# A hybrid decoder layer on one core: the pooling map inside the output weight, loads on other queues, and VectorE's attention step in another order

## The reference, cut to what matters

```python
z = rmsnorm(h, g_attn_norm) @ w_in            # columns: q 512, k 128, v 128, u 512
a = sliding_window_sink_attention(rms(q), rms(k), v, sinks, rel_bias)   # 8 heads, window 128
# four channel groups of 128, trailing means over 2/4/8/16 positions minus the token:
m = concat_g(pooled_g @ w_pool[g]) * pool_scale
h = h + concat(a, m) @ w_out                  # w_out: 1024 x 1024, rows 512.. belong to m
h = h + (silu(hn @ w_gate) * (hn @ w_up)) @ w_down          # hn = rmsnorm(h), d_ff 2816
h = h + sigmoid(rmsnorm(h) @ w_ple_gate) * (p @ w_ple_proj)
```

## Time and profile before

| | us |
|---|---|
| median of 3 runs | 2050.03 (2048.8 to 2052.91) |
| profiled execution, its own time | 2053.4 |
| its span, first to last instruction | 2051.5 |
| TensorE busy | 2011.2 (98%) |
| VectorE busy | 1372.9 (67%) |
| ScalarE busy | 899.7 (44%) |
| GpSimd busy | 406.5 (20%) |
| mean granted TensorE clock | 0.998 of full speed |

### The profile page before, as it was taken

How to read it: one execution, slowest core, us unless ns; L and a number is a source line. 1 busy time by engine, 2 the same in 40 slices (tenths; PEclk the granted TensorE clock), 3 DMA queues, 4 the chain that set the end, 5 groups by cost and what they waited for, 6 DMA issues and landing times.

```text
span 2051.5 us, 26122 instructions
## 1 busy us (share of the span) xinstructions
PE 2011.2 (98%) x9546; PEld 1663.4 (81%) x9546; DVE 1372.9 (67%) x1920; ACT 899.7 (44%) x1460; POOL 406.5 (20%) x508
## 2 busy tenths in 40 slices
PE   8999999999999999999999999999999999999998
PEld 6887878877788888888888878788888888888877
DVE  4696674767696665655888765966566566987663
ACT  4575754657433333333333543533333333334542
POOL 4454644645410000000000220000000000001310
PEclk9999999999999999999999999999999999999999
DMA  7757566364934223225825128432322328352143
GB/s 193 201 180 245 188 236 219 130 236 131 347 127 130 81 72 103 72 72 171 307 62 165 36 72 223 143 119 67 96 85 72 100 79 292 130 159 78 42 134 103
DMA packets 197387, 292.09 MB, mean 142 GB/s; under 512 B 16139, under 2 KB 118452, under 8 KB 195980
## 3 DMA queue, kind: packets, MB, share of 16 engines
q1 hardware_dynamic: 172672, 212.97, 34.1%
q0 software_dynamic: 22176, 76.96, 10.8%
q10 hardware_dynamic: 2412, 0.50, 0.1%
HBM read 223.25 MB, written 67.51 MB: 142 GB/s over the span
## 4 chain that ended last, share of the span: by engine, by line
PE 84%; DVE 6%; DMA 3%; issue 3%; ACT 2%; POOL 1%; SPq 0%; ACTq 0%; DVEq 0%; POOLq 0%
PE bank L2623 13%; PE bank L2627 13%; PE bank L2625 13%; PE bank L2660 7%; PE bank L2661 7%; PE bank L2662 7%; PE bank L2323 4%; PE bank L2325 4%; PE bank L2324 4%; PE bank L2299 2%; PE bank L2301 2%; PE bank L2300 2%; DMA w_parts<-w_split 1%; PE bank L2392 1%; DVE w_lo L1554 1%
## 5 line engine op out<-in xcount | busy, mean ns | idle before, releaser
L2623 PE MATMUL bank<-a_hi,ring_hi 128*128 128x512 f32 x1232 | 479.7, 389 | 1.0 <-DVE ring_lo L1917 0.7
L2627 PE MATMUL bank<-a_hi,ring_lo 128*128 128x512 f32 x1232 | 479.3, 389 | 0.0
L2625 PE MATMUL bank<-a_lo,ring_hi 128*128 128x512 f32 x1232 | 479.3, 389 | 0.0
L2623 PEld LDWEIGHTS bank<-a_hi,ring_hi 128*128 128x128 f32 x1232 | 231.3, 188 | 49.9 <-DVE ring_lo L1917 1.4
L2625 PEld LDWEIGHTS bank<-a_lo,ring_hi 128*128 128x128 f32 x1232 | 231.3, 188 | 48.0
L2627 PEld LDWEIGHTS bank<-a_hi,ring_lo 128*128 128x128 f32 x1232 | 231.3, 188 | 47.8
L2660 PE MATMUL bank<-d_hi 128*128 128x512 f32 x616 | 239.8, 389 | 0.0
L2662 PE MATMUL bank<-d_hi,d_lo 128*128 128x512 f32 x616 | 239.7, 389 | 0.0
L2661 PE MATMUL bank<-d_lo,d_hi 128*128 128x512 f32 x616 | 239.6, 389 | 0.0
L1376 ACT ACTIVATE d_hi<-keep 128x1024 fp32r<-128x1024 f32 x132 | 139.8, 1061 | 201.9 <-PE bank L2662 184.9
L975 POOL DMA_DIRECT2D hidden_T<-hid x88 | 47.6, 541 | 770.4 <-DVE hid L1953 750.7
(11 more groups left out here) (258 smaller groups left out, 3879.9 us busy)
## 6 DMA issues: line engine op xcount, KB each, us to landing
w_parts<-w_split POOLq DMA_DIRECT2D x88, 512.0 KB, 4.8
hidden_T<-hid POOLq DMA_DIRECT2D x88, 256.0 KB, 2.3
raws<-in_w_gate SPq DMA_DIRECT2D x80, 256.0 KB, 4.7
raws<-in_w_up SPq DMA_DIRECT2D x80, 256.0 KB, 5.1
keep<-hidden_T SPq DMA_DIRECT2D x66, 256.0 KB, 3.8
raw<-in_w_ple_gate SPq DMA_DIRECT2D x64, 256.0 KB, 4.2
keep<-in_w_down SPq DMA_DIRECT2D x44, 256.0 KB, 4.4
other<-hidden_T SPq DMA_DIRECT2D x44, 256.0 KB, 6.8
```

The lines of the kernel that those rows point to most:

```text
L2623: mm(dst[:, :], wh[:, g, cols], a_hi[o][:, k, :], start=fresh and k == 0, stop=False, skip_group_check=True)
L2625: mm(dst[:, :], wh[:, g, cols], a_lo[o][:, k, :], start=False, stop=False, skip_group_check=True)
L2627: ins = mm(dst[:, :], wl[:, g, cols], a_hi[o][:, k, :], start=False, stop=k == 3, skip_group_check=True)
```

## The change

- Ahead of everything else in the output projection, z(0) makes W_g · diag(s_g) · Wout_g: POOL loads rows 512 and up of `w_out` (`load_pooled_rows`, 4 x 512 KB), ACT and DVE scale and split them, TensorE multiplies (`mix_rows`, 24 matmuls), ACT copies the banks, POOL stores 4 x 512 KB to `w_mixed`. The out panels with r >= 2 are read from there, and `pool_y` and its copies and waits are gone.
- The constants are issued by POOL, gains 1 and 2 among them; ACT waits for the first gain alone, and issues a small activation at the very start. TensorE runs 12 matmuls on zeroed tiles before its first panel (`WARM`).
- `load_parts` is on SP. Some loads of SP change places (x chunks and h of tile 1, the `load_a` group).
- DVE's attention step: q is staged before `softmax_in`, v at j = 3, the pooled means at steps 4, 7, 11, 15; u copies go behind the hosted step unless the step begins a new pair. ACT keeps a copy of transposed k (`k_raw`), so that TensorE's next transpose waits for ACT and not for DVE.
- In the gate of even tiles the turn of the squares, the sum and the normalisation move one panel later, and ACT splits the panel for r = 1 between the squares.

```diff
STEPS = 4 * NB + LAG_PV
-SUMS_AT = {3: ((0, 0),), 5: ((1, 0), (1, 1)), 7: ((2, 0),), 8: ((2, 1), (2, 2)), 10: ((3, 0), (3, 1)),
-   11: ((3, 2),), 12: ((3, 3),)}
-MEAN_AT = {4: 0, 6: 1, 9: 2, 13: 3}
-REST_AT = {5: 0, 7: 1, 10: 2, 14: 3}
...
+SUMS_AT = {3: ((0, 0),), 5: ((1, 0), (1, 1)), 8: ((2, 0),), 9: ((2, 1), (2, 2)), 12: ((3, 0), (3, 1)),
+   13: ((3, 2),), 14: ((3, 3),)}
+MEAN_AT = {4: 0, 7: 1, 11: 2, 15: 3}
+REST_AT = {5: 0, 8: 1, 12: 2, 16: 3}
+POOLED_HI_AT, POOLED_LO_AT = {10: 0, 11: 1, 12: 2, 13: 3}, {11: 0, 12: 1, 13: 2, 14: 3}
+POOLED_AT, POOLED_COPY_AT = {13: 0, 14: 1, 15: 2, 16: 3}, {14: 0, 15: 1, 16: 2, 17: 3}
+POOLED_STORE_AT = {16: (0, 1), 17: (2,), 18: (3,)}
...
+WARM = 12
...
 kT_hi = sb("kT_hi", [P, (NB + 1) * P], RING0, F32R)
+wo_raw = [sb(f"wo_raw{g}", [P, D], 22 + 4 * g) for g in range(NPOOL)]
+wo_lo = [sb(f"wo_lo{g}", [P, D], 22 + 4 * g, F32R) for g in range(NPOOL)]
...
     def load_out(t, c):
         if t == 0:
+            if c == 0:
+                sp.wait_ge(mixed_stored, 16 * NPOOL)
             load(OUT_AT[t] + c, out_panel(c))
...
             heads = w_out[0:QW, :].rearrange("(j c p) n -> j p c n", j=2, p=HEAD_DIM)
             return [heads[j, :, 2 * r:2 * r + 2, cols] for j in range(2)]
-        return rows(w_out, 2 * r, 2 * r + 2, cols)
+        return rows(w_mixed[:, :], 2 * r - 4, 2 * r - 2, cols)
...
+    def load_parts(i):
+        kept = (10 + i - OUT_AT[1] if OUT_AT[1] <= i < Z_AT[3] else i - Z_AT[2] if i < Z_AT[3] else
+                i - Z_AT[3] if i < OUT_AT[2] else 10 + (i - OUT_AT[2]) % 8)
+        if i == SPLIT_END:
+            sp.wait_ge(lo_done, SPLIT_END)
+        elif i < SPLIT_END + SLOTS_W:
+            sp.wait_ge(panel_used, SPLIT_END)
+            for parity in range(2):
+                sp.wait_ge(parts_stored[parity], 16 * (SPLIT_END - KEPT_FROM))
+        else:
+            sp.wait_ge(panel_used, i - SLOTS_W + 1)
+        sp.wait_ge(parts_stored[kept % 2], 32 * (kept // 2 + 1))
...
+        for part in range(2):
+            sp.dma_start(w_parts[parts_slot(i)][:, part, :].bitcast(F32), w_split[kept, part]
+                           ).then_inc(parts_landed[parts_slot(i)], 16)
...
             else:
-                sp.wait_ge(y_done, 16)
                 sp.wait_ge(attn_lo, 32)
...
     for t in range(NT - 1):
         for c in range(10):
             load_z(t + 1, c)
+            if t == 1 and c == 0:
+                load_parts(Z_AT[2] + 1)
+            if t:
+                load_parts(Z_AT[t + 1] + c + 2)
...
+            if t == 1 and c == 9:
+                for k in range(4):
+                    load_chunk(3, k)
+                for b in range(NB):
+                    load_h(1, b)
...
         for c in range(8):
...
+            if t == 0 and c == 7:
+                load_parts(Z_AT[2])
+            if t:
+                load_parts(OUT_AT[t] + c + 2)
             if t < 2:
                 for k in {3: (4,), 4: (5, 6), 5: (7,)}.get(c, ()):
                     load_chunk(t + 2, k)
...
+        if OUT_AT[3] + c + 2 < ROW_PANELS:
+            load_parts(OUT_AT[3] + c + 2)
...
         if c == 1:
             load_a(0, 0)
+            load_a(0, 2)
+        if c == 2:
             load_a(0, 1)
             load_a(0, 3)
-        if c == 2:
-            load_a(0, 2)
...
     def z_section(t):
...
-            if t == 2 and half == 0:
-                load_parts(Z_AT[2] + 1)
-            if t >= 2 and half % 2 == 0:
-                load_parts(Z_AT[t] + half // 2 + 2)
...
                 if half == 7:
                     store_band()
                     powers(NORM1[0])
+                    load_pooled_rows()
...
+            if t == 0:
+                for g in POOLED_STORE_AT.get(half, ()):
+                    store_mixed(g)
...
-            if t == 0 and half == 14:
-                load_parts(Z_AT[2])
-            if t and half % 2 == 0 and OUT_AT[t] + half // 2 + 2 < ROW_PANELS:
-                load_parts(OUT_AT[t] + half // 2 + 2)
...
+    def load_constants():
+        pool.dma_start(rel_sb[0:N_BUCKETS, :], rel_bias).then_inc(consts, 16)
...
+        pool.dma_start(gains[:, 1, :], g_ffn).then_inc(consts, 16)
+        pool.dma_start(gains[:, 2, :], g_ple).then_inc(consts, 16)
...
+    def load_pooled_rows():
+        pool.wait_ge(consts, CONSTS)
+        for g in range(NPOOL):
+            pool.dma_start(wo_raw[g][:, :], w_out[QW + g * P:QW + (g + 1) * P, :]).then_inc(consts, 16)
...
+    def store_mixed(g):
+        pool.wait_ge(mixed_copied, 2 * g + 2)
+        pool.dma_start(w_mixed[g * P:(g + 1) * P, :], mixed[g][:, :]).then_inc(mixed_stored, 16)
...
     nc.gpsimd.memset(u[:, :, 0:CARRY], 0.0).then_inc(constants_set, 1)
+    load_constants()
...
             act.wait_ge(kcarried, s)
+        if n:
+            act.wait_ge(kstaged, n)
+        nc.scalar.activation(k_raw[:, :], bank[5][:, 0:P], ACT.Copy)
         nc.scalar.activation(kT_hi[:, (b + 1) * P:(b + 2) * P], bank[5][:, 0:P],
...
-    def pool_y_hi(s, g):
-        act.wait_ge(y_done, 4 * s + g + 1)
-        nc.scalar.activation(mix_of(s)[0][:, 4 + g, :], pool_bank(s, g)[:, :], ACT.Copy,
-                             scale=scale_sb[:, g:g + 1]).then_inc(y_hi, 1)
+    def pooled_rows_hi(g):
+        if g == 0:
+            act.wait_ge(consts, CONSTS + 16 * NPOOL)
+        nc.scalar.activation(wo_hi[g][:, :], wo_raw[g][:, :], ACT.Copy,
+                             scale=scale_sb[:, g:g + 1]).then_inc(wp_hi_done, 1)
+    def copy_mixed(g):
+        for e in range(2):
+            act.wait_ge(mixed_bank, 2 * g + e + 1)
+            nc.scalar.activation(mixed[g][:, e * T:(e + 1) * T], mixed_bank_of(g, e)[:, :],
+                                 ACT.Copy).then_inc(mixed_copied, 1)
...
+            if t == 1 and half == 5:
+                act.wait_ge(mixed_stored, 16 * NPOOL)
             for b in COPY_Q_AT[t > 0].get(half, ()):
...
         else:
-            for j in range(4, KC):
-                square_late(g + 1, j)
+            square_late(g + 1, 4)
+            square_late(g + 1, 5)
+            split(ple + 3)
+            square_late(g + 1, 6)
+            square_late(g + 1, 7)
...
-                if split_behind(second, e, r):
+                if split_behind(second, e, r) and (second or e or r):
...
+                    if r == 3:
                         spread(NORM3[g + 1], bank[BS0[1]], spread3)
...
-    act.dma_start(gains[:, 2, :], g_ple).then_inc(gain_landed, 16)
-    act.wait_ge(gain_landed, 48)
+    act.wait_ge(constants_set, 1)
+    nc.scalar.activation(neg_max[:, 0, 0:1], minus_half[:, :], ACT.Copy)
+    act.wait_ge(gain_landed, 16)
...
     for k in range(2):
         square(NORM1[0], k, h[:, k, :], sq)
-    load_constants()
...
+        nc.vector.tensor_tensor(kT_lo[:, cols], k_raw[:, :], kT_hi[:, cols].bitcast(F32),
                                 ALU.subtract).then_inc(kstaged, 1)
...
             dve.wait_ge(bias_landed, 16 * BIAS_LOADS)
+        if j == 3 and b + 1 < NB:
+            stage_q(s, b + 1)
         if has_unit(k, 0):
             first = P if s == 0 and b == 0 else 0
             softmax_in(16 * s + k, j, first)
-        if j == 3 and b + 1 < NB:
-            stage_q(s, b + 1)
...
+        if j == 3 and b < NB:
             stage_v(s, b)
         if j == 1 and b + 1 < NB:
...
-    def pool_y_rest(s, g):
...
+    def pooled_rows_lo(g):
+        dve.wait_ge(wp_hi_done, g + 2)
...
-            for g in U_COPY_AT[t > 0].get(half, ()):
+            fresh = any(has_unit(k, 0) and k % 2 == 0 for _, k in hosted_steps("z", t, half))
+            u_first = fresh or half == 19 or not late
+            for g in U_COPY_AT[t > 0].get(half, ()) if u_first else ():
                 copy_u(t, g)
             if half in QK_MEAN_AT.get(t, {}):
                 qk_mean(t, QK_MEAN_AT[t][half])
             if half == {0: 19, 3: 17}.get(t):
                 qk_normalise(t, 0)
-            if t:
-                for g in POOL_Z_COPY.get(half, ()):
-                    pool_y_rest(t - 1, g)
+            if t == 0 and half in POOLED_LO_AT:
+                pooled_rows_lo(POOLED_LO_AT[half])
+            if t == 1 and half == 5:
+                dve.wait_ge(mixed_stored, 16 * NPOOL)
             hosted("z", t, half, Z_AT[t] + half // 2 + 1 if half % 2 == 0 and late else None)
+            for g in () if u_first else U_COPY_AT[t > 0].get(half, ()):
+                copy_u(t, g)
...
-                    if r == 1:
+                    if r == 2:
                         sum_squares(NORM3[g + 1], bank[BS0[0]])
-                    if r == 2:
+                    if r == 3:
                         normalise3(g + 1, 0)
                         normalise3(g + 1, 1)
                         norm3_lo(g + 1, 0)
-                    if r == 3:
                         norm3_lo(g + 1, 1)
                 if not second and e == 1 and r == 1:
...
-        pe.wait_ge(kstaged, 4 * s + min((k + 1) // PAIRS + 1, NB))
+        pe.wait_ge(k_hi_done, 4 * s + min((k + 1) // PAIRS + 1, NB))
...
```

(38 more changed lines are left out.)

119 lines of the change are left out of this document (39 added, 80 removed).

## The result

The changed kernel takes 2065.85 us (median of 4 runs, 2064.62 to 2070.63) beside 2051.47 for the kernel before (4 runs, 2048.8 to 2054.97): ratio 1.0069, 95% interval [1.0054, 1.0084], 14.2 us slower. 2025.0 was forecast, with a range of 2015 to 2040 and 0.05 for slower. The profiled execution has a span of 2064.4 us.

What follows compares the result with a forecast made beforehand. TensorE, busy 98% of the span, was taken as the bound, so only fewer products or less standing help. The terms -6.4 - 2.3 + 1.0 - 4.0 - 6.5 - 3.0 + 1.0 - 4.8 made -25.0 us: 2050.0 to 2025.0, range 2015 to 2040.

Steps and rivals of the forecast that it cites:

- Step 6: Split-weight loads moved from POOL to SP: -3.0 us of late-load waits, and +1.0 for SP's order, bounds 0 and +4.
- second rival: One queue is too little: split-weight loads behind SP's other transfers each take 11.89 us; 2070 us, chance 0.05.
- Step 1: Pooling maps removed from 16 groups, -12.3 us; 24 products come instead, 5.9 us; net -6.4 us of TensorE.
- Step 2: Kernel start: earlier first panel -1.3 us, zeroed-tile products -2.0, waiting for panel 2 +1.0; sum -2.3 us.
- Step 3: Making the pooled weights in z(0), with 2 MB more to load: +1.0 us, bounds 0 and +5.
- Steps 4 and 5: Step 4: waits on the pooling result go, -4.0 us; step 5: DVE's attention step regrouped, -6.5, bounds 0 and -8.7.
- first rival: Waits move instead of vanishing: the attention step gives -2.5 us, pooled rows cost +5; 2033, up to 2040; chance 0.22.
- Step 7: Gate of tiles 0 and 2: waits on squares and late panels go, -5.1 us, +0.3 for DVE's load; sum -4.8.

Runs made afterwards that it cites:

- order mended: Kernel before with split-weight loads on SP, chunks 4 to 7 ahead, tile 1's h behind the third out panel's load, tile 2's stores together: 2051.2 us, ratio 0.9992.
- rows early: Changed kernel with the pooled rows of the output weight issued by GpSimd at half 4 of z(0): 2062.2 us, ratio 1.0048; other kernels include this edit.
- chunks first: Changed kernel with x chunks 4 to 7 of tile 3 issued ahead of the split weights of out(1)'s panels 2 and 3: 2050.3 us, ratio 0.9991.
- chunks and FFN first: As chunks first, with tile 2's four stores and the FFN's first two panels ahead of split-weight loads in out(3): 2050.4 us, ratio 0.9993.
- combined kernel: Changed kernel with chunks first, tile 1's h behind the third out panel's load, v at j = 2, rows early, tile 2's stores together: 2038.3 us, ratio 0.9929.

## Why the prediction was wrong

**Step 6 failed.** It said that "SP has no arithmetic: I take -3.0", and priced the tie of the chunks to TensorE's panels at +1.0, bounds 0 and +4, by volume: 4 MB against the time to be had. The gain was about right (the waits on these loads fell from 4.0 to 0.5 us with the order mended; the time fell by 1.6 us by the ratio, which the interval doesn't tell from nothing). The price was not: gain and price together measured +17.0 us on the kernel before, where -2.0 was forecast, out(1) grew by 13.8 us and the FFN's first half by 4.3, and most of it isn't volume: the late load made 1.1 us of waiting, VectorE's h and qT_lo 8.9. SP has no arithmetic, but it has waits, and what stood behind them was not costed: chunk 4 stood behind four loads of split weights, the last of which waits for TensorE's third panel of the section; behind the chunk stood ACT's hi part, DVE's lo part, and behind that DVE's addition on which TensorE waits. The text asked for the cost of this order and answered with bytes. (It also counts four waits on these loads in the earlier trace rows; the rows hold three.) The same holds at the end of out(3), where the stores and the FFN's first panels stood behind two such loads.

**The second rival** forecast 2070 for one queue. That the time comes near it is luck, since the reason is another: the split weights were to land in 11.89 us each. They didn't: their median landing in the changed kernel is 4.5 us over 88 transfers (two to a load; 4.8 in the kernel before), and one load was late. The Trainium skill's rule (DMA: Bandwidth & Descriptors, SWDGE vs HWDGE vs iDMA) on queues served in turn explains at most the 4.4 us in out(1), where a load stood behind 3 MB of its own queue. That this wait is 0 to 2.0 us with 1 MB ahead agrees with it. Against it, with the loads on GpSimd's queue the wait was 5.2 us (they were issued at 305.3, behind SP's 3 MB of 300.9 to 304.8), so a queue of its own gave no share that helped here.

**Step 1, products.** The 24 products take 5.5 us in z(0), as worked out (four groups of 1.38 us in the kernel with the rows early), and z(0) grew by 7.3 us in the mean with the rows early. Of the 12.3 us saved, the twelve groups in the z sections cost 5.3 when put back and not 9.2; the likely reason is that they stood where DVE is the late one (9.41 of 10 us busy at 410 to 420 before). The count of products, minus 24 and plus 12, was right, and the price in place was too high.

**Step 2** gave nothing, not -2.3: panel 0 landed at 7.6 ("its own landing isn't shown"), the zero products gave at best two products at the full pace and no time that shows, and TensorE met panel 2 late, as its bound said. **Step 3** cost 3.6 us and not 1.0, inside its bounds: GpSimd issued the rows at 40.0, not at 36, and they landed at 54.1, not 48.

**Steps 4 and 5.** L1772's waits went, as said, and then out(0) and the z sections stood for v and lo of the probabilities: early in out(0) the changed kernel stands 2.6 us for lo, where the kernel before stood 1.8 us on L1772, and out(0) takes 51.4 to 54.5 us in the kernels with the change, 51.3 before. Step 5 read a u copy and the pooling result ahead of a late step as the cause of all of them; in z(2) and z(3) it is the scaling pair for two of the four waits, which went with it, and perhaps the reduction for the others, which no run moved. It gave about 1 us instead of 6.5, if anything. Together this is the first rival, the waits move instead of vanishing.

**Step 7** was right: -5.3 beside -4.8.

Put together with these sizes: +17.0 (6), -5.3 (7), +3.6 (3), 0 (2), -6.4 + 3.9 = -2.5 (1; the four groups in the last two sections taken at full price), about -1 (5), 0 (4) make +11.8, against +14.2 measured. The 2.4 us between are within the intervals (3 us either side for each ratio) and not settled; nor are the shares of steps 1, 3 and 5, each of which is known to 1 to 3 us only. One place where effects don't add up is out(1): it grew by 13.8 us with SP's order alone and by 17.7 in the changed kernel, whose third panel was late by 4.4 us and not 1.1. Step 6 is sure from the other side too: mending SP's order in out(1) took 15.5 us off the changed kernel.

## What to carry to other kernels

When loads move to an engine that "does nothing", write down its whole issue order and, for each transfer, the waits of everything ahead of it; then follow who waits for the last one. Begin with a prefetch that is gated by the consumer's progress behind the loads that are ready now, not ahead of them; then look at what it costs there, since here 3 MB ahead of such a load made it late by 1.1 to 6.8 us, and four stores of 512 KB ahead of one by 1.89. And before pricing a removed product or a removed wait at its full length, look whether the engine that is late there gets anything less to do.

## What the runs showed of the hardware

- In out(1) of the changed kernel one queue carried chunks, h and split weights, 222 GB/s in the mean with a median landing of 4.6 us for 512 KB of split weights; most of what was lost there (9.1 of 13.5 us of waiting) was lost to waits ahead of an issue, the other 4.4 to a load behind 3 MB.
- The zero products kept TensorE at work until 7.4 us; after the stand of 2.6 us behind them, in the changed kernel, two products started at the full pace, and then the pace was 0.43 us, the lower level (1.2 GHz), until 3.9 us after the first; in eight of the twelve kernels with zero products it was the lower level from the first. Over all profiles this stretch lasted 2.7 to 5.7 us with the zero products (twelve) and 2.7 to 6.1 without them (five).
- What a stand costs beyond its length varies from one execution to another: behind the same stand of 2.6 us early in out(0), the section took 53.1 to 53.7 us at a granted clock of 0.97 in four profiles (the changed kernel's among them) and 51.7 and 52.0 at 1.00 in two (chunks first, chunks and FFN first). At 411 to 421 us of the combined kernel the granted clock is 0.83 behind a stand of 2.4 us.
